# HGRN2 trunk: the attention diagonal and its first level of scores formed as elementwise products and summed by a matrix of ones

## What is computed

```python
proj = xn @ w_in
q, fr, v, g = split(proj)
q = silu(q) * HGRN_EXPAND ** -0.5
f = lb + (1 - lb) * sigmoid(fr)
k = 1 - f
# S_t = diag(f_t) S_{t-1} + k_t v_t^T,  o_t = S_t^T q_t
```

## Time and profile before

| | |
|---|---|
| Median of 3 runs | 2339.45 us (2339.4 to 2339.58) |
| The profiled execution's own time | 2340.2 us |
| Its span, first to last instruction | 2338.4 us |
| TensorE matmul busy | 2328.3 us |
| VectorE busy | 1691.0 us |
| ScalarE busy | 1044.3 us |
| Mean granted TensorE clock | 0.999 of full |

### The profile page before, as it was taken

The page is one execution under the profiler, slowest core; times in us unless marked ns, Lnnn a source line. Parts: engine busy times, 40 slices in busy tenths (PEclk is TensorE's granted clock), DMA queues, the critical chain, the costliest instruction groups (busy, mean ns, idle before and its releaser), DMA issues.

```text
span 2338.4 us, 37346 instructions
## 1 busy us (share of the span) xinstructions
PE 2328.3 (100%) x13212; PEld 2049.6 (88%) x13212; DVE 1691.0 (72%) x2147; ACT 1044.3 (45%) x1146; POOL 2.7 (0%) x8
## 2 busy tenths in 40 slices
PE   9999999999999999999999999999999999999998
PEld 8988888888888888888888888888888888888887
DVE  7978788768788788764545666666788788785444
ACT  7344443554444444434444444444444444443443
POOL 0000000000000000000000000000000000000000
PEclk9999999999999999999999999999999999999999
DMA  7555554565656656656565666565656656665664
GB/s 248 159 171 163 164 177 157 175 197 182 192 179 195 188 181 196 191 187 193 185 194 185 190 188 190 185 194 172 201 184 188 197 180 189 193 205 186 192 191 157
DMA packets 410284, 434.93 MB, mean 186 GB/s; under 512 B 13264, under 2 KB 386384, under 8 KB 410064
## 3 DMA queue, kind: packets, MB, share of 16 engines
q1 hardware_dynamic: 409616, 431.53, 59.1%
q10 hardware_dynamic: 576, 2.16, 0.3%
HBM read 431.54 MB, written 2.10 MB: 185 GB/s over the span
## 4 chain that ended last, share of the span: by engine, by line
PE 98%; DMA 1%; DVE 0%; ACT 0%; SPq 0%; issue 0%; DVEq 0%; ACTq 0%
PE acc L1071 54%; PE acc L1081 28%; PE acc L1117 3%; PE acc L1118 3%; PE acc L1116 3%; PE acc L1094 3%; PE acc L1103 1%; PE side L1233 1%; PE side L1212 0%; DMA h<-in_x 0%; DMA raw<-in_hgrn_w_in 0%; PE side L1228 0%; PE side L1063 0%; DVE w_parts L552 0%; PE side L1051 0%; ACT w_parts L333 0%
## 5 line engine op out<-in xcount | busy, mean ns | idle before, releaser
L552 DVE TENSOR_TENSOR w_parts<-raw,w_parts 128x1024 fp32r<-128x1024 f32 x816 | 979.9, 1222 | 578.9 <-PE acc L1081 417.6
L333 ACT ACTIVATE w_parts<-raw 128x1024 fp32r<-128x1024 f32 x816 | 856.4, 1058 | 990.8 <-PE acc L1071 764.0
L1071 PE MATMUL acc<-xn,w_parts 128*128 128x512 f32 x4352 | 1040.1, 391 | 1.4 <-ACT w_parts L333 1.0
L1071 PEld LDWEIGHTS acc<-xn,w_parts 128*128 128x128 f32 x4352 | 799.5, 188 | 156.4 <-issue 1.2
L1081 PEld LDWEIGHTS acc<-xn,w_parts 128*128 128x128 f32 x4352 | 557.5, 191 | 20.4
L1081 PE MATMUL acc<-xn,w_parts 128*128 128x256 f32 x4352 | 566.8, 283 | 0.0
L1071 PE MATMUL acc<-act,w_parts 128*128 128x512 f32 x1216 | 290.6, 391 | 0.0
L1071 PEld LDWEIGHTS acc<-act,w_parts 128*128 128x128 f32 x1216 | 223.5, 188 | 43.3
L1081 PEld LDWEIGHTS acc<-act,w_parts 128*128 128x128 f32 x1216 | 156.0, 191 | 6.0
L1081 PE MATMUL acc<-act,w_parts 128*128 128x256 f32 x1216 | 157.9, 283 | 0.0
L1116 PE MATMUL acc<-w_parts,act 128*128 128x512 f32 x352 | 137.3, 390 | 0.0
(11 more groups left out here) (124 smaller groups left out, 1020.7 us busy)
## 6 DMA issues: line engine op xcount, KB each, us to landing
raw<-in_ffn_w_up SPq DMA_DIRECT2D x352, 512.0 KB, 3.7
raw<-in_ffn_w_down SPq DMA_DIRECT2D x176, 512.0 KB, 4.3
raw<-in_hgrn_w_in SPq DMA_DIRECT2D x128, 512.0 KB, 3.8
raw<-in_sc_w_in SPq DMA_DIRECT2D x96, 512.0 KB, 4.6
raw<-in_hgrn_w_out SPq DMA_DIRECT2D x32, 512.0 KB, 3.9
raw<-in_sc_w_out SPq DMA_DIRECT2D x32, 512.0 KB, 4.2
h<-in_x SPq DMA_DIRECT2D x4, 512.0 KB, 7.8
final_w<-in_final_norm ACTq DMA_DIRECT2D x1, 1024.0 KB, 7.2
```

Source lines behind the costliest of these rows:

```text
L333: nc.scalar.activation(w_parts[:, c % RING, :, 0, :], raw[:, c % RING], ACT.Copy).then_inc(hi_ready, 1)
L552: v.tensor_tensor(w_parts[:, c % RING, :, 1, :], raw[:, c % RING], w_parts[:, c % RING, :, 0, :].bitcast(F32), ALU.subtract).then_inc(lo_r ...
L1071: o = mm(to[:, j, :], w[:, q, 0, j * P:(j + 1) * P], src[:, k * KW + q, :, :].rearrange("p n t -> p (n t)"), start=begin and q == 0, stop= ...
```

## The change

The diagonal and level 0 are no longer matmuls of keys by queries. VectorE forms the elementwise products, `tb = qh * kh` for the diagonal (128x1024) and `kl[:, 0] = (qh * fpre) * kh` for level 0 (128x512). ScalarE copies each to a float32r high part, VectorE subtracts to get the low part, and TensorE multiplies both parts by `sum_ones`, a 128x128 matrix of ones, in float32r matmuls of 512 columns: four for the diagonal, two for level 0. GpSimd fills `sum_ones` once.

Order: the diagonal's stage moves in `PLAN` from behind value chunk 2 to behind chunk 7. Level 0's operands move from VectorE's step 1 to step 0 ahead of the split, together with the making of `qh`; its low part and its prefix come at step 1 ahead of the split. The diagonal's product is made at step 5 behind the split, its high part by ScalarE at step 6 ahead of the split, its low part by VectorE at step 6 behind the split. The two sigmoids of a turn go ahead of ScalarE's split of the same step. Two copies for level 0's keys (L786) and the mirrored keys (L906) fall away.

The diff, with the declarations of semaphores left out:

```diff
@@ -112,9 +112,10 @@
...
 LEVEL, OUTPUT = range(2)
-PLAN = [(2, LEVEL, -1), (3, LEVEL, 0), (5, LEVEL, 1), (6, LEVEL, 2), (8, LEVEL, 3), (10, LEVEL, 4),
+PLAN = [(3, LEVEL, 0), (5, LEVEL, 1), (6, LEVEL, 2), (7, LEVEL, -1), (8, LEVEL, 3), (10, LEVEL, 4),
         (12, LEVEL, 5), (13, LEVEL, 6), (15, LEVEL, 7), (17, OUTPUT, 0)]
 V_GROUP = 2
+PAIR_SPLIT, OWN_SPLIT = 1, 6
 LEAD = 2
@@ -167,6 +168,8 @@
...
         sq_mirror = scratch("sq_mirror", [P, 2, P])
+        sum_ones = scratch("sum_ones", [P, P], F32R)
+        pair_parts = scratch("pair_parts", [P, 2, TG * P], F32R)
         scratch_at.close()
@@ -249,6 +255,7 @@
...
+        own_parts = act[:, DT - TG:DT].rearrange("p j n t -> p (j n t)").rearrange("p (n c) -> p n c", n=2)
         y_tok = h[:].rearrange("p j t -> p (j t)").rearrange("p (b n) -> p b n", b=T // P)
@@ -319,6 +326,7 @@
...
                 nc.gpsimd.memset(t[:], 1.0 if t is ones else 0.0).then_inc(inits, 1)
+            nc.gpsimd.memset(sum_ones[:].bitcast(F32), 1.0).then_inc(inits, 1)
@@ -347,11 +355,13 @@
...
-            def phase_of(phase, pieces, peel_last=False):
+            def phase_of(phase, pieces, peel_last=False, ahead=None):
...
                         for kk, (part, _, _, ends) in enumerate(phase.steps(first, g)):
+                            if ahead:
+                                ahead(i, g, kk)
                             c = phase.c0 + g * phase.cpg + kk
@@ -448,13 +458,25 @@
...
+                if not first:
+                    output_steps(i - 1, g, kk)
+
+            def gates_and_products(i, g, kk):
+
                 if (g, kk) in ((1, 0), (2, 0)):
...
                     nc.scalar.activation(tb[:], ta[:], ACT.Sigmoid).then_inc(gate_sig, 1)
-                if not first:
-                    output_steps(i - 1, g, kk)
-
-            phase_of(HGRN_IN, hgrn)
+                n = (g - V_GROUP) * HGRN_IN.cpg + kk
+                if n == PAIR_SPLIT:
+                    act_e.wait_ge(product_ready, at(i, 2, 1))
+                    nc.scalar.activation(pair_parts[:, 0], kl[:, 0].rearrange("p j t -> p (j t)"), ACT.Copy) \
+                        .then_inc(product_hi_ready, 1)
+                if n == OWN_SPLIT:
+                    act_e.wait_ge(product_ready, at(i, 2, 2))
+                    nc.scalar.activation(own_parts[:, 0], tb[:].rearrange("p j t -> p (j t)"), ACT.Copy) \
+                        .then_inc(product_hi_ready, 1)
+
+            phase_of(HGRN_IN, hgrn, ahead=gates_and_products)
             residual_phase(HGRN_OUT, 0, NORM_FFN, rs_n=1, carry=lambda g, kk: output_steps(HGRN_IN.n - 1, g, kk))
@@ -776,25 +798,30 @@
...
                 q_to = ql[:, buf].rearrange("p j (w n) -> p (j w) n", n=n)
+                if n == 1:
+                    link(v.tensor_tensor(q_to, halves(qh[:], n)[:, :, 1], pre[:, :, 1], ALU.mult), i)
+                    v.tensor_tensor(kl[:, buf].rearrange("p j (w n) -> p (j w) n", n=n), q_to, halves(kh[:], n)[:, :, 0],
+                                    ALU.mult).then_inc(product_ready, 1)
+                    v.memset(su[:, :, 1], 1.0)
+                    mark(v.tensor_copy(su[:, :, 0], pre[:, :, 1]))
+                    return
                 v.tensor_tensor(q_to, halves(qh[:], n)[:, :, 1], pre[:, :, 1], ALU.mult)
...
                 for b in range(T // P):
-                    if n == 1:
-                        o = v.tensor_copy(k_to[:, :, :, b], keys(kh, b, n))
-                    else:
-                        o = v.tensor_tensor(k_to[:, :, :, b], keys(kh, b, n), keys(suf, b, n), ALU.mult)
+                    o = v.tensor_tensor(k_to[:, :, :, b], keys(kh, b, n), keys(suf, b, n), ALU.mult)
                 o.then_inc(qk_ready, 1)
-                if n == 1:
-                    v.memset(su[:, :, 1], 1.0)
-                    mark(v.tensor_copy(su[:, :, 0], pre[:, :, 1]))
-                else:
-                    dve.wait_ge(qk_ready, at(i, 1 + len(LEVELS), m + 2))
-                    shape = [P, TG * T // (2 * n), n]
-                    mark(v.tensor_tensor(su[:, :, 0], su[:, :, 0], pre[:, :, 1, n - 1:n].to_broadcast(shape),
-                                         ALU.mult))
+                dve.wait_ge(qk_ready, at(i, len(LEVELS), m + 1))
+                shape = [P, TG * T // (2 * n), n]
+                mark(v.tensor_tensor(su[:, :, 0], su[:, :, 0], pre[:, :, 1, n - 1:n].to_broadcast(shape), ALU.mult))
+
+            def product_low_parts(i, n, product, parts):
+
+                dve.wait_ge(product_hi_ready, at(i, 2, n + 1))
+                v.tensor_tensor(parts[:, 1], product.rearrange("p j t -> p (j t)"), parts[:, 0].bitcast(F32),
+                                ALU.subtract).then_inc(product_parts_ready, 1)
@@ -892,7 +919,7 @@
...
                 if first and (g, kk) == (1, 0):
-                    dve.wait_ge(inits, 4)
+                    dve.wait_ge(inits, 5)
                     dve.wait_ge(masks_loaded, 16)
@@ -903,15 +930,12 @@
...
                     v.tensor_scalar(kh[:], fpre[:], -1.0, 1.0, ALU.mult, ALU.add)
-                    v.tensor_scalar(kl[:, 1], mirrored(fpre[:, :, P:]), -1.0, 1.0, ALU.mult, ALU.add)
                 if not first:
                     output_sums(i - 1, g, kk)
-                if n == 0:
-
-                    dve.wait_ge(gate_sig, at(i, 3, 2))
-                    v.scalar_tensor_tensor(out=qh[:], in0=ta[:], scalar=float(P) ** -0.5, in1=tb[:],
-                                           op0=ALU.mult, op1=ALU.mult).then_inc(qk_ready, 1)
-                    dve.wait_ge(qk_ready, at(i, 1 + len(LEVELS), 1))
+                if n == OWN_SPLIT - 1:
+                    v.tensor_tensor(tb[:], qh[:], kh[:], ALU.mult).then_inc(product_ready, 1)
+                if n == OWN_SPLIT:
+                    product_low_parts(i, 1, tb[:], own_parts)
@@ -919,15 +943,24 @@
...
                 n = g * HGRN_IN.cpg + kk - 2 * HGRN_IN.cpg
+                if n == 0:
+
+                    dve.wait_ge(gate_sig, at(i, 3, 2))
+                    v.scalar_tensor_tensor(out=qh[:], in0=ta[:], scalar=float(P) ** -0.5, in1=tb[:],
+                                           op0=ALU.mult, op1=ALU.mult).then_inc(qk_ready, 1)
+                    dve.wait_ge(qk_ready, at(i, len(LEVELS), 1))
+                    level_operands(i, 0)
+                if n == PAIR_SPLIT:
+                    product_low_parts(i, 0, kl[:, 0], pair_parts)
                 done = [stage for stage, (after, what, _) in enumerate(PLAN) if what == LEVEL and n == after + 1]
...
                 for after, what, m in PLAN:
-                    if what == LEVEL and 0 <= m < len(LEVELS) - 1 and n == after - LEAD + 1:
+                    if what == LEVEL and 0 <= m < len(LEVELS) - 1 and n == (after - LEAD + 1 if m else 1):
                         prefixes(i, m)
                 for after, what, m in PLAN:
-                    if what == LEVEL and m >= 0 and n == after - LEAD:
+                    if what == LEVEL and m > 0 and n == after - LEAD:
                         level_operands(i, m)
@@ -1223,13 +1256,15 @@
...
-                        pe.wait_ge(qk_ready, at(i, 1 + len(LEVELS), m + 2))
-                        if m < 0:
-                            steps = [lambda to, j=j, b=b: mm(to[:, (2 * j + b) * P:(2 * j + b + 1) * P],
-                                                             kl[:, 1, j] if b else kh[:, j, 0:P], qh[:, j, b * P:(b + 1) * P],
-                                                             start=True, stop=True)
-                                     for j in range(TG) for b in range(2)]
+                        if m < 1:
+                            parts, halves = (own_parts, 2) if m < 0 else (pair_parts, 1)
+                            pe.wait_ge(product_parts_ready, at(i, 2, 1 - m))
+                            steps = [lambda to, c=c, n=n: mm(to[:, c * GC:(c + 1) * GC], sum_ones[:],
+                                                             parts[:, n, c * GC:(c + 1) * GC], start=(n == 0),
+                                                             stop=(n == 1))
+                                     for c in range(halves) for n in range(2)]
                         else:
+                            pe.wait_ge(qk_ready, at(i, len(LEVELS), m + 1))
                             steps = [lambda to, j=j: mm(to[:, j * P:(j + 1) * P], kl[:, m % 2, j], ql[:, m % 2, j],
```

More of the change, by code:

```diff
@@ L240, in trunk @@
         qk_ready = sem("qk_ready")
+        product_ready = sem("product_ready")
+        product_hi_ready = sem("product_hi_ready")
+        product_parts_ready = sem("product_parts_ready")
         final_w_loaded = sem("final_w_loaded")
```

## The result

The changed kernel takes 2366.1 us (median of four), the kernel before 2339.43: 1.0111 times as long, 95% interval 1.0097 to 1.0124. One of the four executions ran at a low clock throughout (2873.4 us, mean granted clock 0.75) and doesn't enter the ratio; the other three lie between 2364.4 and 2366.3. The profiled execution took 2366.33, its span is 2364.5 against 2338.4, 26.1 us more. The forecast was 2361.6 in a range from 2352 to 2369.

What follows compares the result with a forecast made beforehand. The prediction took TensorE to bound the kernel. To the 2339.45 us median it added 22.2 (16.6 for waits of 21.0 less 4.6 saved, plus 5.6 for two clock falls): 2361.6 us, range 2352 to 2369.

Steps and rivals of the forecast that it cites:

- The wait: At the diagonal's stage behind chunk 7, TensorE waits for VectorE's low part: 5.25 us a turn, 21.0 in all.
- the rival with falls in all turns: Clock falls in all four waits, or dearer starts: 27.8 us, 28.6 with the dear end, 2368; chance 0.12, shared with no saving.
- dear operations: VectorE's two new 128x1024 operations at the dear end, 1.30 us as the copy by a mask; adds 0.2 a turn.
- TensorE's saving: Diagonal and level 0 as six float32r matmuls take 1.38 us instead of 2.52: 1.14 a turn, 4.6 in all.
- The anchor: VectorE's split of step 2 starts at 167.8 in the second turn, no later than its release.
- The stretch of VectorE up to the low part: VectorE's work from the split of step 2 to the low part's end: 18.42 us, ending at 186.2.
- The sigmoid ahead of the split at step (1,0): In the forget-gate step it delays a split whose chunk is used four chunks on: hidden, at nothing.
- the cover: At step (1,0), four chunks before use hide the delayed split; without that, a microsecond once a turn.
- The second release: The diagonal's stage also needs level 1's buffer, taken at 184.0; an early low part alone leaves 3.0 us of wait.
- The clock: TensorE's clock falls to half in two of the four waits, at 2.8 us each as upper estimate: 5.6.
- no second wait: After the diagonal's wait, VectorE starts the output gates less far behind TensorE, so no further wait was seen.
- the faster rival: VectorE has slack and the wait at the diagonal vanishes: −4.6 us, 2334.9; chance 0.05, split 0.03 faster, 0.02 the same.

Runs made afterwards that it cites:

- the run with the sigmoids back: The changed kernel with both sigmoids of a turn put back behind ScalarE's split of their step: 2373.16 us, ratio 1.0143 to the kernel before.
- the move alone: The kernel before with only the diagonal's stage moved behind chunk 7, its matmuls still float32 on keys and queries: 2350.23 us, ratio 1.0045.
- the filler run: The changed kernel with 22 extra 512-column matmuls on TensorE ahead of the diagonal's wait in each turn: 2357.52 us, ratio 1.0076 to the kernel before.
- behind chunk 8: The changed kernel with the diagonal's stage between the halves of chunks 8 and 9, ahead of level 3, plus one ordering wait on VectorE: 2345.69 us.
- the run with GpSimd: The changed kernel with the diagonal's stage behind chunk 14 and its product and low part made by GpSimd instead of VectorE: 2352.03 us, ratio 1.0052.
- the low part first: The changed kernel with the diagonal's low part made at step 6 ahead of level 1's take and the split: 2360.53 us, ratio 1.009.

## Why the prediction was right

The mechanism is the one forecast: TensorE waits for VectorE's low part in every turn, and the clock falls in the wait. Against the forecast's terms, 21.0 of waits − 4.6 saved + 5.6 of clock, the trace has 22.3 − 4.6 + 8.4. The wait was 1.3 us short and the clock 2.8. The measured time lies closer to the rival with falls in all turns (2368, or 2367.25 without its dear operations) than to the forecast of 2361.6.

- **TensorE's saving.** Right. From the value group's start to the end of chunk 7 it takes 188.05 − 163.53 = 24.5 us in place of 26.8; the prediction had 24.7 (180.99 − 156.27). The output gates start 5.15 us later in the turn (195.46 − 163.53 = 31.93, against 26.78), not 4.15: of the difference, 0.95 is the stage itself, which takes 1.87 at half clock instead of 0.92.
- **The anchor.** Right, nearly a tie: VectorE begins the split of step 2 at 175.07, and had no idle time in front of it. But the tie was less harmless than written: the run with the sigmoids back shows steps 0 and 1 without any slack.
- **The stretch of VectorE up to the low part.** Summed 18.42 us, measured 18.4; the two new operations take 1.22 us each, as the split. The wait: 5.25 forecast (its terms give 5.23), 5.37 in three turns. All four: 21.0 forecast, 22.3 measured. The first turn's 6.16 is the next point. One reading was off without effect: the prediction lets VectorE's split of step 6 start at 184.9, where by its own terms the low part starts; the split starts at 183.8 (191.08 in the trace, 7.26 later in the run), which is still behind ScalarE's at 182.9.
- **The sigmoid ahead of the split at step (1,0).** Costed at nothing, and wrong for the first turn. There the forget gates' sigmoid waits for the root and the scaling, the split now waits behind it, its raw slot is free later, and so is the transfer that reuses it. ScalarE in the first turn of the changed kernel:

```profile
41.09 1.06 ACT L468 ACTIVATE tb<-ta 128x1024 f32<-128x1024 f32 x1 [1.79 <-DVE ta L617]
...
51.49 1.06 ACT L341 ACTIVATE w_parts<-raw 128x1024 fp32r<-128x1024 f32 x1 [2.21 <-DMA raw<-in_hgrn_w_in]
...
54.42 1.06 ACT L341 ACTIVATE w_parts<-raw 128x1024 fp32r<-128x1024 f32 x1 [0.92 <-DMA raw<-in_hgrn_w_in]
```

  In the kernel before this wait for a transfer is 1.4 us, once; here it is 2.2 and 0.9, and VectorE scales the queries 3.8 us after the value group's start (58.76 against 54.95), not 2.3 as in the kernel before (57.80 against 55.49 in the same turn). With the sigmoids back it is 2.3 again (57.59 against 55.28), and the first turn's wait isn't longer than the others'. The price is the 0.8 us by which 6.16 is over 5.37, near the microsecond that the prediction had named as the price if the cover went. That run moves both sigmoids, so the part of this one alone is argued from the timeline and not shown by itself.
- **The second release.** Right. The prediction had 3.0 us of wait for the buffer, with the product made and the low part out of the way. With the low part ahead of the take it is some 1.2 more (4.25, and L847 ends it); with neither of the two operations, in the move alone, it is some 1.2 less (1.84). Each operation takes 1.14 from start to start.
- **The clock.** The mechanism was right; its count and its price were off, in opposite directions, and that they partly cancel is luck. Forecast: two falls at 2.8, 5.6 us. Measured: four falls, 8.4 by the account, 8.6 by the filler run, so 2.1 each. The likeliest case should have been the rival with all four, at a lower price. The 2.8 came from the start of the run, the upper estimate; part of each low stretch passes while TensorE still waits and costs nothing. The granted clock shows it by turn: it was low for 23.9 us in all, of which TensorE was past its wait for 4.5, 3.2, 5.9 and 3.9 us in the four turns, and half of that is 8.7. So one fall costs from 1.6 to 2.9 us.
- **What "no second wait" and the faster rival overlooked.** In the changed kernel no further wait was seen, since the wait of 5.4 us let VectorE catch up. Where the wait is taken away, the lateness comes out at level 4 or 6. The faster rival therefore never gave 2334.9: without the wait the time is 2343.

The step behind both is one: the prediction costed VectorE's two new operations only for their place in front of the diagonal, not for the levels behind it. In the forecast case this cost nothing; in the faster rival it is worth 8 us.

## What to carry to other kernels

Where one engine is the bound by the page, sum the stretch of the second engine before taking work off the first: here a trade of 4.6 us of TensorE for 2.3 us a turn of VectorE loses 3.5 us even at the best place found, because VectorE has no idle time to spare there (none from 169.5 to 213.6 in the second turn of the kernel before). A stage put into a list that takes turns on two buffers changes what the stage itself and the next two stages wait for; look at whose buffer has to be taken first. And a wait of TensorE costs its length plus what the clock does after it: here 5.4 plus 2.1 us on average, and filler matmuls won the second part back where the wait itself stayed.

## What the runs showed that was not expected

- In the profiled executions the clock fell with waits of 1.74 to 2.4 us in six of twelve turns (behind chunk 8, the move alone, and the run with GpSimd, two turns of each), and in every one of twelve turns with waits of 4.2 us or more (the changed kernel, the low part first, the sigmoids back). With waits of 1.4 us and less it never fell. In the six turns with a short wait it fell 0.3 to 1.5 us after TensorE had begun to work again. At the same length of wait, 1.84 us in one run, it fell in the third turn and held in the second and fourth. In what these turns differ, no run here tells; one execution of each kernel was profiled.
- VectorE's two-input operation of 0.69 us took 2.77 while GpSimd ran one.
